# Pre norms of a chain of fp32 layers: products of x times the norm's gain, a token's factor applied out of PSUM, squares from PSUM, and one program without barriers

## The chip, the core and the metric

The kernel runs on one core of a Trainium2 chip. The metric is the device time of one execution in microseconds (us); lower is better. Its engines are TensorE (PE) with its weight loads (PEld), VectorE (DVE), ScalarE (ACT), GpSimd (POOL) and SyncE (SP), which issues the transfers. They run their own programs and meet at semaphores.

## The reference

x is 512 tokens by 1024 columns in float32. Two `hybrid_layer`s run over it and then one `hybrid_layer_2`, each between norms:

```python
def rms_norm(x, g):
    y = xf * lax.rsqrt(jnp.mean(xf * xf, axis=-1, keepdims=True) + EPS)
    return (y * g.astype(jnp.float32)).astype(x.dtype)

def hybrid_layer(x, ...):
    h = rms_norm(x, g_mix_pre)
    u = h @ w_in
    ...                         # attention, convolution and retention of slices of u
    mix = jnp.concatenate([y_att, y_conv, y_ret], axis=-1) @ w_out
    x = x + rms_norm(mix, g_mix_post)
    h = rms_norm(x, g_mlp_pre)
    f = jnp.square(jax.nn.relu(h @ w_up)) @ w_down
    return x + rms_norm(f, g_mlp_post)

def hybrid_layer_2(x, mem, ...):
    x = x + 0.5 * swiglu_ffn(rmsnorm(x, ffn1_norm), ffn1_w_in, ffn1_w_down)
    u = rmsnorm(x, mix_norm)
    proj = u @ w_in
    ...                         # a state space scan, dilated attention, attention over mem, gates
    x = x + merged @ w_out
    x = x + 0.5 * swiglu_ffn(rmsnorm(x, ffn2_norm), ffn2_w_in, ffn2_w_down)
    return x

def swiglu_ffn(x, w_in, w_down):
    a, b = jnp.split(x @ w_in, 2, axis=-1)
    return (jax.nn.silu(a) * b) @ w_down
```

The result is `rmsnorm` of it with `final_norm`. A *pre norm* stands ahead of a projection (`g_mix_pre`, `g_mlp_pre`, `ffn1_norm`, `ffn2_norm`), a *post norm* behind one. The factor `rsqrt(mean)` of a norm is one number per token, so it can be applied to the rows of `h @ w` as well as to h.

## The kernel before

**Layout.** Everything is feature-major: x is `x_sb`, 8 tiles k of 128 features by 512 tokens. A projection takes a tile's features from the weights and leaves 128 outputs by 512 tokens in one PSUM bank; there are four (`gemm0` to `gemm3`), taken in turns by twos.

**Products.** An fp32 product is three matmuls of rounded parts: high by high, high by low, low by high. The weights come in *pieces* of 256 columns and 8 tiles of rows, 1 MB each. A piece is loaded by SP into `w_raw` (two buffers, `load_block` L325), rounded by ACT to `w_hi` (`round_block`, L344), and DVE makes `w_lo` (`rest_block`, L353). A piece has two output tiles m; `product` (L356, its matmuls at L384) runs m outside and k inside: 48 matmuls. It waits for `w_lo` once (semaphore `w_rest`) and, in a stage's first piece, for each tile of h (`h_ready`). Two pieces are in work at a time: a buffer is loaded again when both parts of the piece in it are made, and rounded again when the products of the piece before are done (`units`). `g_free` counts the banks read out.

**A norm** is a chain across the engines: squares on ACT (`norm_squares`, L456); their sum over features on PE by products with a matrix of ones into PSUM (`norm_add`, L461, and L482), 8 of them, or 3 where POOL has added the first six squares (`squares_added`, L471); ACT's root of one row (`norm_rooted`, L510); PE turns the row into columns (`norm_turn`, L498); DVE's reciprocal (L515); PE spreads it over all partitions (`norm_spread`, L504). Then, for a post norm, DVE scales each tile of `out_sb` by gain and factor (L520) and adds it to x (L549). For a pre norm DVE scales each tile of x by gain and factor into `out_sb` (L520), ACT rounds it to `h_hi` (L527), DVE subtracts to `h_lo` (L538), and the product of that tile may start.

**Stages of a layer.** 14 pieces of w_in with attention, convolution and retention woven in, 4 pieces of w_out, and twice 8 pieces of up and 8 of down. Up is relu by ACT out of PSUM (L1005), square on DVE (L1216), rounding. The second down half's tiles are copied from PSUM by ACT to `part` (L1017) and added by DVE (L1239). In the third part each FFN is 11 pairs of pieces (a silu on the first, a copy of the second, their product on DVE), then down with `part` and an add (L2043).

**Order around the norms.** All queues are written by hand. At w_out's and down's end PE does `norm_of_added` for the post norm and then `norm_total` for the pre norm, which both run before any product of the next stage. The two layers are one loop (`nc.Fori(0, DEPTH)`) with a block in it; at its end, and behind the start block, `clear_counts` puts all semaphores to zero between barriers, and the weight buffers' first two pieces, loaded and rounded ahead, are told to the next block by `head_start`. The third part is a block of its own. The start block loads constants and x, then weights; it does the first pre norm's root and both roundings.

## Time and profile before

| | us |
|---|---|
| three runs, median (lowest, highest) | 2854.04 (2852.43, 2858.58) |
| the profiled execution | 2853.72 |
| its span, first to last instruction | 2851.9 |
| PE busy in the span | 2710.3 (95%) |
| DVE, ACT, POOL busy | 1291.4 (45%), 1015.0 (36%), 287.8 (10%) |

The mean granted clock of PE is 0.972 of full speed. The boundaries between stages, where a pre norm stands, with PE's busy time in each (a stretch from about the last tile of the old stage to the second piece of the new one):

| stretch, us | boundary | length | PE busy |
|---|---|---|---|
| 0 to 57 | start | 57 | 36.0 |
| 324 to 375 | w_out to up, layer 0 | 51 | 41.9 |
| 701 to 762 | layer 0 to layer 1 | 61 | 42.1 |
| 1029 to 1082 | w_out to up, layer 1 | 53 | 44.5 |
| 1408 to 1466 | layer 1 to third part | 58 | 43.3 |
| 2458 to 2500 | w_out2 to ffn2 | 42 | 32.8 |

How to read the rows below: a row of the page's first part is an engine's busy time with its share of the span. A busy PE isn't PE at its peak: matmuls are pipelined, each is shown with 0.39 us at the full clock, and they start 0.2265 us apart. A granted clock of 0.50 is the lower of its two levels, 1.2 of 2.4 GHz.

### The profile page before, as it was taken

How to read it: one execution, taken by the hardware profiler on the slowest of the kernel's cores; microseconds unless marked ns; L12 is line 12 of the kernel's file. 1: busy time of each engine (PE TensorE's matmuls, PEld its weight loads, DVE VectorE, ACT ScalarE, POOL GpSimd, SP SyncE). 2: the span in 40 equal slices, each digit the busy share in tenths (PEclk: the TensorE clock that was granted, in tenths of full speed). 3: DMA queues.
4: the chain of work that ended last, by engine and by line, in shares of the span. 5: the costliest groups of instructions: out<-in, count | busy, mean ns of one | idle time of the engine just before them, and what ended most of it. 6: DMA issues, size and time to landing. Idle time of an engine off the chain costs nothing. (4 is left out here: it accounts for less than half of the span.)

```text
span 2851.9 us, 31899 instructions
## 1 busy us (share of the span) xinstructions
PE 2710.3 (95%) x12330; PEld 2122.2 (74%) x12330; DVE 1291.4 (45%) x1666; ACT 1015.0 (36%) x1433; POOL 287.8 (10%) x276
## 2 busy tenths in 40 slices
PE   7999899999799989999989999999999998899998
PEld 5875688887587568888768888777777666688886
DVE  4754442342574444233343333478773446333322
ACT  3333332232333333233333333433235453334322
POOL 0000000001000000000100000067540230000000
PEclk9999999999899989999999999999999999999999
DMA  3310122322231012322122322412131024122222
GB/s 123 126 53 30 59 82 95 104 88 74 72 122 45 30 59 88 103 89 103 59 82 96 103 92 91 168 60 74 53 132 52 30 75 162 61 101 90 94 91 80
DMA packets 41443, 241.88 MB, mean 85 GB/s; under 512 B 5232, under 2 KB 5744, under 8 KB 18416
## 3 DMA queue, kind: packets, MB, share of 16 engines
q1 hardware_dynamic: 41056, 239.25, 24.4%
q8 instruction: 77, 1.26, 0.2%
q0 software_dynamic: 272, 1.05, 0.1%
q14 instruction: 38, 0.31, 0.0%
HBM read 231.90 MB, written 8.39 MB: 84 GB/s over the span
## 5 line engine op out<-in xcount | busy, mean ns | idle before, releaser
L353 DVE TENSOR_TENSOR w_lo<-w_raw,w_hi 128x2048 fp32r<-128x2048 f32 (+3 forms) x219 | 464.2, 2120 | 850.4 <-ACT w_hi L344 850.2
L384 PE MATMUL gemm<-h_hi,w_hi 128*128 128x512 f32 x1936 | 777.7, 402 | 47.9 <-DVE h_lo L538 44.0
L384 PE MATMUL gemm<-h_hi,w_lo 128*128 128x512 f32 x1936 | 760.5, 393 | 0.0
L384 PE MATMUL gemm<-h_lo,w_hi 128*128 128x512 f32 x1936 | 760.5, 393 | 0.0
L344 ACT ACTIVATE w_hi<-w_raw 128x2048 fp32r<-128x2048 f32 (+3 forms) x219 | 383.5, 1751 | 257.5 <-PE gemm L384 254.3
L384 PEld LDWEIGHTS gemm<-h_hi,w_hi 128*128 128x128 f32 x1936 | 367.0, 190 | 139.0 <-issue 46.1
L384 PEld LDWEIGHTS gemm<-h_hi,w_lo 128*128 128x128 f32 x1936 | 367.2, 190 | 78.2
L384 PEld LDWEIGHTS gemm<-h_lo,w_hi 128*128 128x128 f32 x1936 | 368.1, 190 | 71.8 <-issue 1.7
L384 PE MATMUL gemm<-f_hi,w_hi 128*128 128x512 f32 x512 | 199.4, 389 | 0.0
L384 PE MATMUL gemm<-f_hi,w_lo 128*128 128x512 f32 x512 | 199.4, 389 | 0.0
L384 PE MATMUL gemm<-f_lo,w_hi 128*128 128x512 f32 x512 | 199.4, 389 | 0.0
L1770 ACT ACTIVATE swi<-gemm 128x512 f32<-128x512 f32 x88 | 52.7, 598 | 285.3 <-PE gemm L384 285.3
L384 PE MATMUL gemm<-g_hi,w_hi 128*128 128x512 f32 x352 | 137.5, 390 | 0.0
L384 PE MATMUL gemm<-g_lo,w_hi 128*128 128x512 f32 x352 | 137.1, 389 | 0.0
L384 PE MATMUL gemm<-g_hi,w_lo 128*128 128x512 f32 x352 | 137.1, 389 | 0.0
L1216 DVE TENSOR_TENSOR tt<-tt 128x512 f32<-128x512 f32 x64 | 44.1, 689 | 156.3 <-ACT tt L1005 156.3
L1005 ACT ACTIVATE tt<-gemm 128x512 f32<-128x512 f32 x64 | 38.3, 599 | 207.7 <-PE gemm L384 207.7
L384 PEld LDWEIGHTS gemm<-f_hi,w_lo 128*128 128x128 f32 x512 | 96.1, 188 | 19.9
L384 PEld LDWEIGHTS gemm<-f_hi,w_hi 128*128 128x128 f32 x512 | 96.1, 188 | 19.9
L384 PEld LDWEIGHTS gemm<-f_lo,w_hi 128*128 128x128 f32 x512 | 96.1, 188 | 19.9
L471 POOL TENSOR_TENSOR sq_f<-sq_f 128x512 f32<-128x512 f32 x20 | 31.1, 1557 | 778.0 <-ACT sq_f L456 776.8
L384 PE MATMUL gemm<-w_hi,h_hi 128*128 128x256 f32 (+1 forms) x352 | 107.3, 305 | 0.0
(370 smaller groups left out, 3614.4 us busy)
## 6 DMA issues: line engine op xcount, KB each, us to landing
w_raw<-in_w SPq DMA_DIRECT2D x171, 1024.0 KB, 4.8
w_raw<-in_w SPq DMA_DIRECT2D x16, 768.0 KB, 4.2
w_raw<-in_w SPq DMA_DIRECT2D x16, 640.0 KB, 3.8
w_raw<-in_w SPq DMA_DIRECT2D x18, 512.0 KB, 3.7
bias_t<-in_att_bias SPq DMA_DIRECT2D x2, 1536.0 KB, 9.2
decay_t<-in_c_decay SPq DMA_DIRECT2D x2, 1536.0 KB, 8.2
x_sb<-in_x SPq DMA_DIRECT2D x4, 512.0 KB, 5.4
x_kept<-x_sb SPq DMA_DIRECT2D x1, 2048.0 KB, 11.0
```

Of the source, the lines that this page charges most:

```text
L344: act.activation(w_hi[:, b.slot, 0:size], w_raw[:, b.slot, 0:size], ACT.Copy).then_inc(S["w_rounded"], 1)
L353: dve.tensor_tensor(w_lo[:, b.slot, 0:size], w_raw[:, b.slot, 0:size], w_hi[:, b.slot, 0:size].bitcast(F32), ALU.subtract).then_inc(S["w_r ...
L384: mm = pe.matmul(dst, lhs, rhs, start=b.first and k == 0 and j == 0, stop=b.last and k == b.kt - 1 and j == 2)
L471: pool.tensor_tensor(sq[:, 0, :], sq[:, 0, :], sq[:, k, :], ALU.add).then_inc(S["sq_added"], 1)
L1005: act.activation(tt[:, 2 * j + m, :], tile_of(b, m), ACT.Relu).then_inc(S["g_free"], 1)
L1216: dve.tensor_tensor(tt[:, 2 * j + m, :], tt[:, 2 * j + m, :], tt[:, 2 * j + m, :], ALU.mult).then_inc(S["f_sq"], 1)
L1770: act.activation(swi[:, 2 * j + m, :], tile_of(b, m), (ACT.Silu, ACT.Copy)[j]).then_inc(S["g_free"], 1)
```

## The change

Four things change, in one edit of the whole program.

1. *Pre norms at the head of a stage* (mix_pre, mlp_pre, ffn1, ffn2). ACT makes `h_hi` from x times gain (`raw_hi`), DVE `h_lo` (`raw_rest`), as soon as a tile of x is there, with no token factor. `opening` puts the products of the stage's first two pieces one tile k at a time, alternating between the pieces, and the norm's sum, turn and spread among the last of them. ACT copies the spread factor into `rs` (`open_act`). POOL adds six of the squares in all of these norms. The pre norms of the mix in the third part and of mem stay as they were.
2. *The factor* is applied to the results. In the layers' w_in, DVE multiplies the first two pieces out of PSUM, POOL the q, k, rq, rk and rg tiles in SBUF (`by_root`), and the token-major pieces get it as ACT's scale. In up, DVE takes relu and factor out of PSUM in one instruction and ACT squares. In the third part's FFNs DVE multiplies the first piece by the factor out of PSUM, ACT takes the silu, POOL multiplies by the factor again, and DVE multiplies with the second piece out of PSUM.
3. *PSUM is read directly* for the squares of w_out and for the adds of the last down tiles (`part` goes), which DVE now does before the next `rest_block`.
4. *One program.* The layers are written out twice in one block, each with offsets for its semaphore counts (`counts`), the pieces of all parts have one numbering, the layers' parameters have two buffers, and `clear_counts`, `head_start` and the barriers go. At the start SP issues the parameters and the first piece before x.

The new functions, and the places that use them (indentation and counts that only follow are left out):

```diff
+        def raw_hi(act, k, gain):
+            act.activation(h_hi[:, k, :], x_sb[:, k, :], ACT.Copy, scale=gain[:, k:k + 1]).then_inc(S["norm_hi"], 1)
+        def raw_rest(dve, j, k, gain):
+            dve.wait_ge(S["norm_hi"], KD * j + k + 1)
+            dve.scalar_tensor_tensor(out=h_lo[:, k, :], in0=x_sb[:, k, :], scalar=gain[:, k:k + 1],
+                                     in1=h_hi[:, k, :].bitcast(F32), op0=ALU.mult,
+                                     op1=ALU.subtract).then_inc(S["h_ready"], 1)
+        def post_norm_dve(dve, i, gain, normed, j, next_gain):
             norm_inverse(dve, i)
-            for k in range(KD + 1):
-                if k < KD:
+            for k in range(KD):
                     norm_scale(dve, i, k, out_sb, out_sb, gain)
                 if k:
-                    dve.wait_ge(S["normed"], KD * i + k)
-                    dve.tensor_tensor(x_sb[:, k - 1, :], x_sb[:, k - 1, :], out_sb[:, k - 1, :],
-                                      ALU.add).then_inc(S["x_done"], 1)
-        gains = {n: par[:, 8 * i:8 * i + 8] for i, n in enumerate(("mix_pre", "mix_post", "mlp_pre", "mlp_post"))}
-        conv_w = par[:, 32:94].rearrange("p (j t) -> p j t", j=2)
-        conv_b, ln_g, ln_b = par[:, 94:96], par[:, 96:98], par[:, 98:100]
+                    raw_rest(dve, j, k - 1, next_gain)
+                dve.wait_ge(S["normed"], normed + k + 1)
+                dve.tensor_tensor(x_sb[:, k, :], x_sb[:, k, :], out_sb[:, k, :], ALU.add).then_inc(S["x_done"], 1)
+            raw_rest(dve, j, KD - 1, next_gain)
+        def split_x(act, i, sq, gain, wait, tiles=range(KD)):
+            for k in tiles:
+                act.wait_ge(wait[0], wait[1] + k + 1)
+                raw_hi(act, k, gain)
+                act.activation(sq[:, k, :], x_sb[:, k, :], ACT.Square).then_inc(S["squares"], 1)
+        OPENING = [(q, k) for k in range(5) for q in range(2)] + [
+            (0, 5), (0, 6), (0, 7), "sum", (1, 5), "turn", (1, 6), "spread", (1, 7)]
+        FIRST_OPENING = [(0, k) for k in range(6)] + [
+            (1, 0), (1, 1), (0, 6), (0, 7), "sum", (1, 2), (1, 3), (1, 4), "turn", (1, 5), (1, 6), "spread", (1, 7)]
+        def opening(pe, pair, i, sq, ready, order=OPENING):
+            waited = 0
+            for at in order:
+                if at == "sum":
+                    added_total(pe, i, sq)
+                elif at == "turn":
+                    norm_turn(pe, i)
+                elif at == "spread":
+                    norm_spread(pe, i)
+                else:
+                    b, k = pair[at[0]], at[1]
+                    if k == 0:
+                        pe.wait_ge(S["w_rest"], b.n + 1)
+                    if k >= waited:
+                        pe.wait_ge(S["h_ready"], ready + k + 1)
+                        waited = k + 1
+                    wh, wl = view(w_hi, b), view(w_lo, b)
+                    for m in range(b.tiles):
+                        if k == 0 and b.need[m]:
+                            pe.wait_ge(S["g_free"], b.need[m])
+                        c = slice(m * P, (m + 1) * P)
+                        dst = bank[b.bank + m][:]
+                        pe.matmul(dst, wh[:, k, c], h_hi[:, k, :], start=k == 0, stop=False)
+                        pe.matmul(dst, wh[:, k, c], h_lo[:, k, :], start=False, stop=False)
+                        mm = pe.matmul(dst, wl[:, k, c], h_hi[:, k, :], start=False, stop=k == KD - 1)
+                        if k == KD - 1:
+                            mm.then_inc(S["units"], 1)
+        def open_act(act, i, b):
+            round_block(act, b.n + 2)
+            norm_rooted(act, i)
+            act.wait_ge(S["norm_spread"], i)
+            act.activation(rs[:], t_ps[:], ACT.Copy).then_inc(S["rs_ready"], 1)
+        def open_dve(dve, i, b):
+            norm_inverse(dve, i)
+            rest_block(dve, b.n + 2)
...
+        def begin_sync(sp):
+            sp.dma_start(pars[0][:, 0:100], A["par1"][0]).then_inc(first_par_in, 16)
+            load_block(sp, plan[0])
+            load_x(0)
             sp.dma_start(ones[:], A["c_ones"]).then_inc(consts_in, 16)
             sp.dma_start(ident[:], A["c_ident"]).then_inc(consts_in, 16)
+            load_x(2)
+            load_x(4)
+            load_block(sp, plan[1])
+            load_x(6)
...
-                    norm_of_added(pe, 1, 0, sq_f)
-                    norm_total(pe, 2, out_sb)
+            norm_of_added(pe, N0 + 1, sq_f)
...
+                    opening(pe, plan1[first.i:first.i + 2], N0 + 2, out_sb, cnt("h_ready", 2 * KD))
...
-                    norm_of_added(pe, 3, KD - 3, sq_f)
-                    norm_total(pe, 4, sq_f)
+            norm_of_added(pe, N0 + 3, sq_f)
...
+            def by_root(b, tiles):
+                for m in range(b.tiles):
+                    pool.wait_ge(S["g_free"], b.t0 + m + 1)
+                    pool.tensor_tensor(tiles[m], tiles[m], rs[:], ALU.mult).then_inc(S["pool_r"], 1)
...
-                    squares_added(pool, 1, 0, sq_f)
-                    squares_added(pool, 3, KD - 3, sq_f)
+            squares_added(pool, N0 + 1, sq_f)
+            squares_added(pool, N0 + 2, out_sb)
+            squares_added(pool, N0 + 3, sq_f)
+            squares_added(pool, N0 + 4, sq_f)
...
-                    norm_squares(act, 3, out_sb, sq_f, wait=(S["part_done"], 0), tiles=(KD - 2, KD - 1))
-                    norm_rooted(act, 3)
-
-                    round_next(act, 0, plan1)
-                    norm_squares(act, 4, x_sb, sq_f, wait=(S["x_done"], KD))
-                    norm_rooted(act, 4)
-                    round_next(act, 1, plan1)
+            for b in plan1[DOWN[1]:DOWN[1] + 8]:
+                round_block(act, b.n + 2)
+                k = (b.i - DOWN[1]) // 2 * 2 - 2
+                if not b.last and k >= 0:
+                    norm_squares(act, N0 + 3, out_sb, sq_f, wait=(S["g_free"], last_down), tiles=(k, k + 1))
+            norm_squares(act, N0 + 3, out_sb, sq_f, wait=(S["g_free"], last_down), tiles=(KD - 2, KD - 1))
+            norm_rooted(act, N0 + 3)
+            split_x(act, N0 + 4, sq_f, next_gain, (S["x_done"], cnt("x_done", KD)))
...
+                for m in range(2):
+                    dve.wait_ge(S["units"], t.u(b.u0 + m + 1))
+                    dve.scalar_tensor_tensor(out=tt[:, 2 * j + m, :], in0=tile_of(b, m), scalar=0.0, in1=rs[:],
+                                             op0=ALU.max, op1=ALU.mult).then_inc(S["g_free"], 1)
...
+                        dve.tensor_tensor(out_sb[:, k, :], out_sb[:, k, :], tile_of(b, m),
+                                          ALU.add).then_inc(S["g_free"], 1)
+                rest_block(dve, b.n + 2)
...
-            clear_counts()
...
+            def silu_by_root(base):
+                with pool.Fori(0, 11) as i:
+                    for m in range(2):
+                        pool.wait_ge(S["silu"], base + i * 2 + (m + 1))
+                        pool.tensor_tensor(swi[:, m, :], swi[:, m, :], rs[:], ALU.mult).then_inc(S["silu_r"], 1)
```

How the order of the instructions changes on two engines. First DVE between w_out and up of a layer (L353 and after it L357 are the weights' low parts, L520 and then L494 the scale, L549 and then L534 the add to x, L538 and then L522 the low part of h). Before, the post norm's rows and the beginning of the pre norm's:

```order
L353 TENSOR_TENSOR w_lo<-w_raw,w_hi 128x2048 x4
L515 RECIPROCAL tiny<-mixed 128x4
L520 SCALAR_TENSOR_TENSOR out_sb<-out_sb,par_sb,turned 128x512 x2
L549 TENSOR_TENSOR x_sb<-x_sb,out_sb 128x512
L520 SCALAR_TENSOR_TENSOR out_sb<-out_sb,par_sb,turned 128x512
...
L549 TENSOR_TENSOR x_sb<-x_sb,out_sb 128x512 x2
L515 RECIPROCAL tiny<-mixed 128x4
L520 SCALAR_TENSOR_TENSOR out_sb<-x_sb,par_sb,turned 128x512 x2
L538 TENSOR_TENSOR h_lo<-out_sb,h_hi 128x512
```

And after the change:

```order
L357 TENSOR_TENSOR w_lo<-w_raw,w_hi 128x2048 x4
L489 RECIPROCAL tiny<-mixed 128x4
L494 SCALAR_TENSOR_TENSOR out_sb<-out_sb,par_sb,turned 128x512
L534 TENSOR_TENSOR x_sb<-x_sb,out_sb 128x512
L494 SCALAR_TENSOR_TENSOR out_sb<-out_sb,par_sb,turned 128x512
L522 SCALAR_TENSOR_TENSOR h_lo<-x_sb,par_sb,h_hi 128x512
L534 TENSOR_TENSOR x_sb<-x_sb,out_sb 128x512
...
L534 TENSOR_TENSOR x_sb<-x_sb,out_sb 128x512
L522 SCALAR_TENSOR_TENSOR h_lo<-x_sb,par_sb,h_hi 128x512
L489 RECIPROCAL tiny<-mixed 128x4
```

The low part of h has moved from behind the second reciprocal to one row behind each add of the post norm.

The same place on PE, the sums and the first products, before:

```order
L482 MATMUL mixed<-sq_f_86,ones_sb_57 128x512
L461 MATMUL mixed<-sq_f_86,ones_sb_57 128x512 x2
L498 MATMUL mixed<-ones_sb_57,rs_60 128x1 x4
L504 MATMUL turned<-ident_sb_56,tiny_62 128x128 x4
L461 MATMUL mixed<-out_sb_55,ones_sb_57 128x512 x8
L498 MATMUL mixed<-ones_sb_57,rs_60 128x1 x4
L504 MATMUL turned<-ident_sb_56,tiny_62 128x128 x4
L384 MATMUL gemm0<-h_hi_53,w_hi_50 128x512
```

After, first where the opening begins and then its last part:

```order
L472 MATMUL mixed<-ones_sb_57,rs_60 128x1 x4
L478 MATMUL turned<-ident_sb_56,tiny_63 128x128 x4
L572 MATMUL gemm0<-h_hi_53,w_hi_50 128x512
L573 MATMUL gemm0<-h_lo_54,w_hi_50 128x512
L574 MATMUL gemm0<-h_hi_53,w_lo_51 128x512
L572 MATMUL gemm1<-h_hi_53,w_hi_50 128x512
...
L465 MATMUL mixed<-out_sb_55,ones_sb_57 128x512
L437 MATMUL mixed<-out_sb_55,ones_sb_57 128x512 x2
L572 MATMUL gemm2<-h_hi_53,w_hi_50 128x512
...
L472 MATMUL mixed<-ones_sb_57,rs_60 128x1 x4
...
L478 MATMUL turned<-ident_sb_56,tiny_63 128x128 x4
```

The eight ones-products of the pre norm have become three (L465, L437), and they stand 78 rows of products behind the start of the stage, before the second piece's last three tiles.

The third place is DVE from the last piece of w_out2 into ffn2 (L2043 and then L2456 are the adds to x). Before:

```order
L353 TENSOR_TENSOR w_lo<-w_raw,w_hi 128x2048
L2043 TENSOR_TENSOR x_sb<-x_sb,part 128x512 x2
L515 RECIPROCAL tiny<-mixed 128x4
L520 SCALAR_TENSOR_TENSOR out_sb<-x_sb,par_sb,turned 128x512 x2
L538 TENSOR_TENSOR h_lo<-out_sb,h_hi 128x512
```

And after:

```order
L357 TENSOR_TENSOR w_lo<-w_raw,w_hi 128x2048
L2456 TENSOR_TENSOR x_sb<-x_sb,gemm 128x512 x2
L522 SCALAR_TENSOR_TENSOR h_lo<-x_sb,par_sb,h_hi 128x512 x2
L489 RECIPROCAL tiny<-mixed 128x4
L357 TENSOR_TENSOR w_lo<-w_raw,w_hi 128x2048
L2131 TENSOR_TENSOR swi<-gemm,rs 128x512 x2
L2138 TENSOR_TENSOR swi<-gemm,swi 128x512 x2
```

The adds now read the banks themselves, so a bank is free behind the weights' low part and the add; each pair of adds is followed by two low parts of h.

## Rows read from the trace of the kernel before

**Rows 1.** The page's head line and the busy share of PE, first part.

```profile
span 2851.9 us, 31899 instructions
...
PE 2710.3 (95%) x12330; PEld 2122.2 (74%) x12330; DVE 1291.4 (45%) x1666; ACT 1015.0 (36%) x1433; POOL 287.8 (10%) x276
```

**Rows 2.** Waits of PE by releaser: us in total, times, longest.

```profile
PE gemm L384 <- DVE h_lo L538: 44.0, 20, 12.9
```

**Rows 3.** Stretches: length; PE, PEld, DVE, ACT, POOL busy (count); clock; DMA; GB/s.

```profile
375.00:700.00 325.00, 325.00 (x1435) 269.23 (x1434) 109.74 (x95) 99.89 (x109) 9.11 (x5) 1.00 0.27 94
701.00:762.00 61.00, 42.08 (x152) 27.69 (x151) 28.36 (x38) 21.65 (x29) 0.00 (x0) 0.80 0.16 54
```

**Rows 4.** Timeline (start, us, engine, line), layer 0, w_out to up; idle before in brackets.

```profile
324.27 0.60 ACT L886 ACTIVATE out_sb<-gemm 128x512 f32<-128x512 f32 x1 [4.84 <-PE gemm L384]
325.44 1.98 PE L461 MATMUL mixed<-sq_f,ones_sb 128*128 128x512 f32 x4 [0.34 <-ACT sq_f L456]
...
327.60 0.66 ACT L510 ACTIVATE rs<-mixed,eps_c 1x512 f32<-1x512 f32 x1
...
330.17 1.16 PE L504 MATMUL turned<-ident_sb,tiny 128*128 128x128 f32 x8 [0.81 <-DVE tiny L515]
331.37 1.41 DVE L520 SCALAR_TENSOR_TENSOR out_sb<-out_sb,par_sb,turned 128x512 f32<-128x512 f32 x2 [1.25 <-PE turned L504]
332.69 0.68 DVE L549 TENSOR_TENSOR x_sb<-x_sb,out_sb 128x512 f32<-128x512 f32 x1
...
349.20 0.77 PE L384 MATMUL gemm<-h_hi,w_hi 128*128 128x512 f32 x1 [2.32 <-DVE h_lo L538]
...
374.78 0.60 ACT L1005 ACTIVATE tt<-gemm 128x512 f32<-128x512 f32 x1 [4.84 <-PE gemm L384]
```

**Rows 5.** Timeline, layer 0 to layer 1.

```profile
708.03 1.41 DVE L520 SCALAR_TENSOR_TENSOR out_sb<-out_sb,par_sb,turned 128x512 f32<-128x512 f32 x2 [1.65 <-PE turned L504]
...
736.40 0.76 PE L384 MATMUL gemm<-h_hi,w_hi 128*128 128x512 f32 x1 [12.85 <-DVE h_lo L538]
...
761.99 0.60 ACT L886 ACTIVATE cg<-gemm 128x512 f32<-128x512 f32 x1 [4.84 <-PE gemm L384]
```

**Rows 6.** Stretches of PE alone: length, busy (matmuls), clock, DMA, GB/s.

```profile
736.40:739.40 3.00, 3.00 (x7) 0.50 0.92 358
739.40:742.40 3.00, 2.90 (x9) 0.71 0.67 276
```

**Rows 7.** Timeline, the other boundaries: start's end; layer 1; third part.

```profile
57.16 0.60 ACT L886 ACTIVATE cg<-gemm 128x512 f32<-128x512 f32 x1 [4.84 <-PE gemm L384]
...
1037.46 0.75 DVE L520 SCALAR_TENSOR_TENSOR out_sb<-out_sb,par_sb,turned 128x512 f32<-128x512 f32 x1 [2.17 <-PE turned L504]
...
1081.82 0.60 ACT L1005 ACTIVATE tt<-gemm 128x512 f32<-128x512 f32 x1 [4.84 <-PE gemm L384]
...
1415.52 0.75 DVE L520 SCALAR_TENSOR_TENSOR out_sb<-out_sb,par_sb,turned 128x512 f32<-128x512 f32 x1 [2.10 <-PE turned L504]
...
1466.22 0.60 ACT L1770 ACTIVATE swi<-gemm 128x512 f32<-128x512 f32 x1 [4.84 <-PE gemm L384]
```

**Rows 8.** Transfers, 0 to 20 us: GB/s in 40 slices of 0.5 us.

```profile
GB/s 0 0 0 77 109 106 205 291 360 418 360 365 324 385 381 373 328 323 257 428 442 360 492 442 360 475 410 407 287 139 19 0 0 0 0 0 0 0 0 0
```

**Rows 9.** Timeline, w_out2 to ffn2.

```profile
2458.68 0.60 ACT L1756 ACTIVATE part<-gemm 128x512 f32<-128x512 f32 x1 [3.80 <-PE gemm L384]
2459.17 1.90 ACT L344 ACTIVATE w_hi<-w_raw 128x2048 fp32r<-128x2048 f32 x1
2461.11 2.29 DVE L353 TENSOR_TENSOR w_lo<-w_raw,w_hi 128x2048 fp32r<-128x2048 f32 x1 [7.38 <-ACT w_hi L344]
...
2499.55 0.60 ACT L1770 ACTIVATE swi<-gemm 128x512 f32<-128x512 f32 x1 [4.84 <-PE gemm L384]
```

**Rows 10.** Timeline, POOL and DVE side by side in layer 0's w_out.

```profile
314.59 2.73 POOL L471 TENSOR_TENSOR sq_f<-sq_f 128x512 f32<-128x512 f32 x2 [8.86 <-ACT sq_f L456]
...
316.87 2.60 DVE L353 TENSOR_TENSOR w_lo<-w_raw,w_hi 128x2048 fp32r<-128x2048 f32 x1 [8.99 <-ACT w_hi L344]
```

More of the change, by code:

```diff
@@ L75, in __init__, with number @@
         self.group, self.narrow = group, narrow
-def number(pieces, tok_tiles=None):
+def number(*parts):
+    pieces = []
+    for part in parts:
+        for i, b in enumerate(part):
+            b.i = i
+            pieces.append(b)
     units = 0
@@ L214, in third_pieces @@
     ffn("ffn2")
[L215 to L216 removed]
+    return out, start
 def build(nc, ins, outs):
     A = ins
[L221 to L222 removed]
+    third_part, AT2 = third_pieces()
+    plan = number(*(layer_pieces() for _ in range(DEPTH)), third_part)
+    n1 = (len(plan) - len(third_part)) // DEPTH
+    plan2 = plan[DEPTH * n1:]
     with ExitStack() as ctx:
```

3018 lines of the change are left out of this document (1527 added, 1491 removed).

## The prediction

> **What bounds the kernel now.** I read the head line and the busy shares first [rows 1]: TensorE (PE) works through 95% of a span of 2851.9 us and no other engine through half of it, so only time in which PE waits, or works on something that goes away, can be won. Then the waits by releaser: PE's largest is that of the products at line 384 for the low part of h at line 538, 44.0 us in 20 waits [rows 2]. Then two stretches [rows 3]: from 375 to 700 us (up and down of a layer) PE is busy throughout at a full clock; from 701 to 762 (a layer's end and the next one's first two pieces) for 42.1 of 61 us, at a mean clock of 0.80. The time lies at the boundaries, so I read those row by row.
>
> At each boundary I use anchors that stay in the changed kernel: T0, where ScalarE (ACT) takes the last-but-one tile of the old stage out of PSUM; t0, the first scale of the post norm on VectorE (DVE); and the end, the take-out of the last-but-one tile of the new stage's second piece. From w_out to up in layer 0 [rows 4] T0 is 324.27, then come three ones-products (0.99 each: 1.98 for two), the root at 327.60, the spread at 330.17, t0 at 331.37. Eight times scale and add follow, in which PE only sums the pre norm's squares; then root, turn and spread again; the first product starts at 349.20, the end is 374.78. Of these 50.5 us the two pieces need 21.7: 96 matmuls at 325.00/1435 = 0.2265 us each [rows 3].
>
> **The change, part by part.**
>
> *An opening.* Products take x times gain, which is there as soon as x is, and the pre norm's sum, turn and spread stand among the products of the second piece. On PE, from its first product to the end: 96 x 0.2265 = 21.7; three ones-products, 3.0 (eight become three, GpSimd (POOL) adds the first six squares); the spread 1.16 [rows 4] and the turn, eight small loads too, as much: 27.0. After a long wait PE's clock is at its lower level (1.2 of 2.4 GHz): at 736.40, 16 products take 6.00 us at granted clocks of 0.50 and 0.71 where 3.6 would do [rows 6], 2.4 lost. The new idle time ahead is shorter, so I take 1.7: **28.7** an opening. Bounds: 27.0 (no slow clock, and nothing below it, since the same products remain) and 31 (slow for twice as long).
>
> *Its start.* Per tile DVE makes a scale, a low part (new, two SBUF operands, bounded by the 0.68 of the add) and the add: 0.70 + 0.68 + 0.68, about 2.05 us; ACT makes the high part (0.60 as a copy) and the square beside it. The first low part stands behind scale, add, high part and the next scale: t0 + 2.9. PE eats 2.72 us of products a tile (12 of them), so DVE keeps ahead; tiles 5 to 7 are taken at 1.36 each, where its lead is 2 us at a full clock, 4 at a slow start.
>
> *B0, w_out to up, layer 0.* Squares now come from PSUM ahead of the copy: 0.55 sooner. Start 331.37 - 0.55 + 2.9 = 333.7, end 362.4 for 374.78: **12.3**. *B1, the same in layer 1* [rows 7]: 1037.46 - 0.55 + 2.9 + 28.7 = 1068.5 for 1081.82: **13.3**.
>
> *C0, layer 0 to layer 1.* t0 708.03, first product 736.40, end 761.99 [rows 5]; the barrier, the clearing of the counts and the branch lie in the 12.85 us that PE waits there, and go too. ACT now rounds a piece (1.90) ahead of the last squares, 0.75 on the root. 708.03 + 0.75 + 2.9 + 28.7 = 740.4: **21.6**. *C1, layer 1 to the third part* [rows 7]: 1415.52 + 32.35 = 1447.9 for 1466.22: **18.3**.
>
> *A, the start.* Before, all squares, a root and two roundings stand ahead of the products, end 57.16 [rows 7]. After, gains and first piece are asked for first. Summing the half-microsecond slices [rows 8], some 1.3 MB are in by 6.6 us, and piece 0 (1.05 MB, asked for first) with them; then ACT's rounding 1.90, DVE's low part 2.29 [rows 9], and x's low part 0.7: start 11.6, end 40.3: **16.9**, give or take 2 for what the queue does with another order.
>
> *E, w_out2 to ffn2.* T0 2458.68, end 2499.55 [rows 9]. h's tiles are made while w_out2 still runs, and PE goes on with tile 0 of piece 0 at once. Then it waits for piece 1's low part (rounding from T0 on, 1.90, then 2.29 on DVE, so T0 + 4.3) and for banks that the last adds free behind it on DVE (T0 + 5.6). That leaves some 3.8 idle: T0 + 3.8 + 27.0 + 0.4 = 2489.9: **9.7**.
>
> *F, the final norm.* Its adds read PSUM and save one copy, 0.60: **0.5**.
>
> *The factor elsewhere.* POOL multiplies q, k, rq, rk and rg by it (15 tiles a layer), DVE the first two pieces and up (relu and factor in one instruction). In the third part's FFNs a pair's first piece goes DVE product 0.7, ACT silu 0.6, POOL product 1.4 twice: done 4.8 us after that piece, where the second piece ends after 10.9 (48 x 0.2265). From there DVE's two products, ACT's rounding, two low parts and the next weights' low part are about 5.8 of the next 10.9. DVE and ACT are busy for a third of the long stretch (109.74 and 99.89 of 325 us [rows 3]). So **0**, hidden behind PE's products; if the cover were gone it is rival 3. The unrolled layers, the offsets of the counts and the one numbered plan add nothing on an engine in use: **0**.
>
> Sum: 12.3 + 13.3 + 21.6 + 18.3 + 16.9 + 9.7 + 0.5 = 92.6. From the profiled execution's 2853.7 (1.8 over its span, 0.3 below the runs' median) that is **2761 us**.
>
> **A rule against this change.** Two POOL adds of squares, 1.37 us each, end at 317.32; a weights' low part that DVE starts at 316.87 takes 2.60 us, the like one at 2461.11 with POOL idle 2.29 [rows 9, 10]: 0.31 lost on 0.45 of overlap. The changed kernel puts five such adds beside each opening's DVE chain. The Trainium skill, "SBUF — State Buffer", section "Who interferes with whom", says that a DVE instruction with two SBUF inputs and a GpSimd instruction that reads SBUF shut each other out, the one issued second waiting in full. By that rule the five adds would stop the chain for as long as they last; the row agrees in sign and roughly in size. What that gives is rival 1.
>
> **The rivals.**
>
> (1) *Openings starved or cold.* If the five adds (6.8 us) stop DVE for their whole length, its chain loses 6.8 against a lead of 4: up to 2.8 in each of B0, B1, C0, C1, +11, so 2772. If only the clash of the two SBUF kinds counts (two thirds of DVE's time), 4.5 against 4: +2. And if the clock stays low for 8 us, six openings lose some 1.7 more: +10, 2771. Both in part: 2767 to 2780. For it: rows 10, and the mean clock of 0.80 [rows 3]; against: in half of its time POOL waits for the next square. Chance 0.28.
>
> (2) *More is won.* PE's wait ahead of the products shrinks from 12.85 us [rows 5] to about 2.5; if the clock is then up, 5 x 1.7 = 8.5 less, and the start may be 2 sooner: 2749 to 2755. Against it: after 2.32 us of wait the product at 349.20 still takes 0.77 and not 0.39. Chance 0.17.
>
> (3) *POOL becomes the third part's bound: slower.* There are 22 FFN pairs, and each now goes through POOL. A pair loses time from the point at which its POOL products end 10.9 + (10.9 - 5.8) = 16 us after its first piece, where they end at 4.8 now. To eat 92.6 us it takes 4.2 a pair more, 20.2 us: a POOL product of 9 us each and not 1.37 [rows 10]. Past that, it is slower than before, over 2860. Chance 0.02; as much again, 0.02, that such a product takes 8 to 9 us and the gain is just eaten.
>
> (4) *The products do not open.* Piece 1's low part, or the four banks that two interleaved pieces hold at once, could be late until every tile is there anyhow. Then PE starts at t0 + 17.3 (8 x 2.05 + 0.9) and ends 27.0 later: B0 nothing, B1 0.7, C0 761.99 - 753.1 = 8.9, C1 5.6, start 11, E 9.7, together 36: 2818. Against it: the post norm waits for the sum of squares anyhow, and into the 7.1 us from T0 to t0 a rounding and a low part (1.90 + 2.29) fit. Chance 0.01.
>
> **How the numbers follow.** The forecast, 2755 to 2767, gets 0.50 and is the likeliest: 2761. To hold 8 in 10 the range goes to 2749 (rival 2, the clock up in all openings and an early start) and to 2780 (rival 1; openings at their bound of 31 are +14). What it leaves out are rivals 3 and 4 and the far ends of 1 and 2. A measurement of this kernel can tell about 0.2%, 6 us, from no change: faster by more than that 0.50 + 0.28 + 0.17 + 0.01 = 0.96, within it 0.02, slower 0.02.
>
> **What would show it.** After: the first product of up some 9.5 us behind T0, and products from there without a gap of over 0.5 us; the three ones-products within the second piece; from t0 to the end 31.6 us in B and C where C0 had 54.0; no barrier at layer ends; the start's end near 40; PE busy throughout between boundaries. Wrong: PE waiting for h's low part at tiles 5 to 7 beside POOL adds (rival 1), a clock of 0.50 for over 4 us (rival 1) or never (rival 2), PE waits inside the third part's FFN pairs (rival 3), a first product 17 us behind t0 (rival 4). The forecast fails as a whole if ends move less than starts.

## The result, and the profile after

The changed kernel takes 2774.35 us (median of 4 runs, 2773.67 to 2774.83) for 2853.89 us: a ratio of 0.9718, 95% interval 0.9703 to 0.9734. That is 79.5 us less, where 92.6 were forecast, and it lies in the range of 2749 to 2780: not in the forecast's own stretch of 2755 to 2767, but in the one of 2767 to 2780 that the first rival had. The profiled execution took 2773.67 us, its span:

```profile
span 2771.8 us, 31517 instructions
...
PE 2669.7 (96%) x12280; PEld 2109.0 (76%) x12280; DVE 1342.1 (48%) x1670; ACT 944.5 (34%) x1331; POOL 428.3 (15%) x375
```

PE is busy 40.6 us less than in [rows 1] and idle for about as much less; POOL has half as much again to do. The waits of PE by releaser (total, times, longest):

```profile
PE gemm L572 <- DVE h_lo L522: 17.6, 9, 12.5
PE gemm L572 <- issue: 12.6, 4, 3.2
```

The 44.0 us of [rows 2] are 17.6, of which 12.5 are the start. The 12.6 us put down to "issue" are four waits of 3.15 between a post norm's spread and the first product.

One correction to the prediction's words before the numbers: it calls its anchors T0 and end the take-out of the *last-but-one* tile. The rows show the *last* tile (all 96 products of the two pieces lie ahead of 374.78, and the ones-products begin at 324.07). The arithmetic used them so, and nothing in the sum changes. Below, T0 is the start of the first ones-product of the post norm, and the end is the first product of the stage's third piece; both are 0.2 us ahead of those of the rows. A's T0 is the start of the span. E has no post norm; its T0 is where w_out2's last product gives way, 2458.5 before and 2386.7 after.

| boundary | T0 to end, before | after | won | forecast |
|---|---|---|---|---|
| A, start | 57.0 | 41.8 | 15.2 | 16.9 |
| B0, w_out to up, layer 0 | 50.5 | 41.7 | 8.8 | 12.3 |
| C0, layer 0 to 1 | 60.8 | 42.2 | 18.6 | 21.6 |
| B1, w_out to up, layer 1 | 52.4 | 41.7 | 10.7 | 13.3 |
| C1, layer 1 to third part | 58.0 | 42.0 | 16.0 | 18.3 |
| E, w_out2 to ffn2 | 40.9 | 32.5 | 8.4 | 9.7 |
| all | | | 77.7 | 92.1 |

Between the boundaries another 2.4 us went, most of them in layer 1's w_in (1.7) and the third part (1.2); no wait of PE there changed by as much, and what they are stays open. They may be chance: in pe_sum below, whose edit doesn't touch it, the third part between its two openings is 5.0 us longer than here. So the order of the terms came out as forecast, and every one was taken too large. The boundary w_out to up of layer 0 shows why. Its timeline, first up to the first product (start, duration, engine, line; idle time before in brackets):

```profile
309.12 1.02 PE L465 MATMUL mixed<-sq_f,ones_sb 128*128 128x512 f32 x2
...
312.08 0.66 ACT L484 ACTIVATE rs<-mixed,eps_c 1x512 f32<-1x512 f32 x1
...
314.66 2.07 PE L478 MATMUL turned<-ident_sb,tiny 128*128 128x128 f32 x8 [0.82 <-DVE tiny L489]
...
316.78 0.75 DVE L494 SCALAR_TENSOR_TENSOR out_sb<-out_sb,par_sb,turned 128x512 f32<-128x512 f32 x1 [2.17 <-PE turned L478]
...
319.04 0.75 DVE L522 SCALAR_TENSOR_TENSOR h_lo<-x_sb,par_sb,h_hi 128x512 fp32r<-128x512 f32 x1
...
319.89 0.77 PE L572 MATMUL gemm<-h_hi,w_hi 128*128 128x512 f32 x1 [3.15 <-issue]
```

The spread takes 2.07 us for 1.16 in [rows 4]: PE's clock has already fallen there (the granted clock is 0.50 from 314.6). It is at its lower level for the first products as well (stretches: length; PE, PEld, DVE, ACT, POOL busy; clock):

```profile
319.89:322.89 3.00, 3.00 (x7) 2.42 (x8) 2.87 (x4) 1.24 (x2) 1.15 (x1) 0.50 0.00 0
322.89:325.89 3.00, 3.00 (x10) 2.33 (x10) 2.87 (x4) 1.24 (x2) 1.10 (x2) 0.68 0.00 0
```

And this is DVE's chain beside POOL's adds, and what PE sees of it later:

```profile
319.70 0.69 DVE L534 TENSOR_TENSOR x_sb<-x_sb,out_sb 128x512 f32<-128x512 f32 x1
...
321.74 1.32 POOL L454 TENSOR_TENSOR out_sb<-out_sb 128x512 f32<-128x512 f32 x1 [21.34 <-ACT out_sb L542]
321.85 1.77 DVE L534 TENSOR_TENSOR x_sb<-x_sb,out_sb 128x512 f32<-128x512 f32 x1
323.54 0.73 DVE L494 SCALAR_TENSOR_TENSOR out_sb<-out_sb,par_sb,turned 128x512 f32<-128x512 f32 x1
...
338.19 0.50 PE L572 MATMUL gemm<-h_hi,w_hi 128*128 128x512 f32 x1 [0.74 <-DVE h_lo L522]
...
340.33 0.50 PE L572 MATMUL gemm<-h_hi,w_hi 128*128 128x512 f32 x1 [0.48 <-DVE h_lo L522]
```

The add to x at 319.70 takes 0.69 us; the one at 321.85, issued 0.11 behind POOL's, takes 1.77: it stands until POOL is done at 323.06 and then runs. This isn't chance. POOL's add waits for ACT's square, which ends just as DVE comes to the add of x, so it falls on that add in five tiles of each opening. PE waits for tiles 6 and 7: 0.74 and 0.48 us idle in these rows, and 1.5 to 1.7 us an opening in all four by the starts of its products.

At the start ACT's table load has moved behind the first wait (before, it ran at 0.73 us, under the transfers). Of A's missing 1.7 us it is 1.0, as the run `ends` shows below; the rest lies in the opening, 29.3 us for 28.7:

```profile
6.12 1.28 ACT L348 ACT_TABLE_LOAD   x1 [6.12 <-DMA w_raw<-in_w]
7.41 1.91 ACT L348 ACTIVATE w_hi<-w_raw 128x2048 fp32r<-128x2048 f32 x1
```

### The profile page after: what moved, and what is told of

Read it like the earlier page. It is cut to its first block, busy times and chain, and to the rows that moved or that the text cites. A ratio compares the mean times of both kernels' runs of the same rounds, so it can differ in the third digit from the quotient of the medians.

```text
span 2771.8 us, 31517 instructions
## 1 busy us (share of the span) xinstructions
PE 2669.7 (96%) x12280; PEld 2109.0 (76%) x12280; DVE 1342.1 (48%) x1670; ACT 944.5 (34%) x1331; POOL 428.3 (15%) x375
## 4 chain that ended last, share of the span: by engine, by line
PE 87%; DVE 7%; ACT 4%; issue 2%; DMA 0%; ACTq 0%; DVEq 0%; SPq 0%
PE gemm L388 71%; ACT w_hi L348 2%; DVE x_sb L534 2%; PE score L742 1%; PE mixed L763 1%; DVE w_lo L357 1%; PE gemm L572 1%; DVE h_lo L522 1%; PE mixed L1601 1%; ACT h_hi L517 1%; PE gemm L574 1%; PE score L1590 1%; PE gemm L573 1%; PE turned L753 1%; PE mixed L437 1%
## 5 line engine op out<-in xcount | busy, mean ns | idle before, releaser
L357 DVE TENSOR_TENSOR w_lo<-w_raw,w_hi 128x2048 fp32r<-128x2048 f32 (+3 forms) x225 | 473.2, 2103 | 651.0 <-ACT w_hi L348 650.7
L388 PE MATMUL gemm<-h_hi,w_lo 128*128 128x512 f32 x1744 | 679.9, 390 | 0.0
L388 PE MATMUL gemm<-h_lo,w_hi 128*128 128x512 f32 x1744 | 679.1, 389 | 0.0
L348 ACT ACTIVATE w_hi<-w_raw 128x2048 fp32r<-128x2048 f32 (+3 forms) x225 | 393.4, 1749 | 438.9 <-PE gemm L388 401.0
L388 PEld LDWEIGHTS gemm<-h_hi,w_hi 128*128 128x128 f32 x1744 | 327.6, 188 | 75.8 <-issue 6.1
L388 PEld LDWEIGHTS gemm<-h_hi,w_lo 128*128 128x128 f32 x1744 | 327.3, 188 | 69.2
L388 PEld LDWEIGHTS gemm<-h_lo,w_hi 128*128 128x128 f32 x1744 | 327.8, 188 | 66.1 <-issue 1.7
L454 POOL TENSOR_TENSOR sq_f<-sq_f 128x512 f32<-128x512 f32 x30 | 47.7, 1590 | 750.6 <-ACT sq_f L432 653.1
L1749 POOL TENSOR_TENSOR swi<-swi,rs 128x512 f32<-128x512 f32 x44 | 56.9, 1295 | 411.3 <-ACT swi L1857 411.3
L572 PE MATMUL gemm<-h_hi,w_hi 128*128 128x512 f32 x192 | 85.7, 446 | 33.9 <-DVE h_lo L522 17.6
L388 PE MATMUL gemm<-w_lo,h_hi 128*128 128x256 f32 (+1 forms) x352 | 106.0, 301 | 0.0
## 6 DMA issues: line engine op xcount, KB each, us to landing
x_kept<-x_sb SPq DMA_DIRECT2D x1, 2048.0 KB, 10.9
```

Source lines behind the costliest of these rows:

```text
L348: act.activation(w_hi[:, b.slot, 0:size], w_raw[:, b.slot, 0:size], ACT.Copy).then_inc(S["w_rounded"], 1)
L357: dve.tensor_tensor(w_lo[:, b.slot, 0:size], w_raw[:, b.slot, 0:size], w_hi[:, b.slot, 0:size].bitcast(F32), ALU.subtract).then_inc(S["w_r ...
L388: mm = pe.matmul(dst, lhs, rhs, start=b.first and k == 0 and j == 0, stop=b.last and k == b.kt - 1 and j == 2)
L454: pool.tensor_tensor(sq[:, 0, :], sq[:, 0, :], sq[:, k, :], ALU.add).then_inc(S["sq_added"], 1)
L572: pe.matmul(dst, wh[:, k, c], h_hi[:, k, :], start=k == 0, stop=False)
L1749: pool.tensor_tensor(swi[:, m, :], swi[:, m, :], rs[:], ALU.mult).then_inc(S["silu_r"], 1)
```

## The experiments

Eleven kernels ran, each timed against the kernel before in turns on one chip. Times are medians in us; the ratio is to the kernel before. The changed kernel itself has 0.9718. The kernels ran on three chips, on which the kernel before took 2852.7 us (pe_sum, sq_r, warm, best0), 2854.0 (warm_sq, ends, serial, blocks) and 2849.7 (pool3, pool6, best1), and 2853.9 beside the changed kernel; so across these groups the ratios compare, and times only to some us. Where times are close I go by the places in the profile. Two causes were in question for what was missing, and they can hide each other: POOL's adds hold DVE up (lockout), and PE's clock falls because PE stands idle ahead of an opening (idle clock). The plain rival to both is that the chain from ACT to DVE is just slower than I took it.

### pe_sum: POOL's adds out of the openings

```diff
                 if at == "sum":
-                    added_total(pe, i, sq)
+                    for k in range(KD):
+                        norm_add(pe, i, sq, k)
...
-            squares_added(pool, N0 + 2, out_sb)
...
-            squares_added(pool, N0 + 4, sq_f)
```

> The changed kernel, but in the four openings behind a post norm PE sums all eight squares itself and GpSimd adds none. Theory (GpSimd's add shuts DVE out for its whole length): the add to x goes back from 1.78 to 0.69 us in all tiles, the tile period of DVE's chain from 3.24 to about 2.1 us, and PE no longer waits for h's low part at tiles 6 and 7 (1.6 us an opening now). PE pays five more ones-products of 0.72 us: 3.6 - 1.6 = 2.0 more in each of four, so about 2782 us. Rival (the chain is slow of itself, by its own waits from ACT to DVE and back): the waits stay and the time is 4 x 3.6 up, 2789 us.

Measured: 2786.07 us, ratio 0.9762 (0.9746 to 0.9779). By time alone this lies between the theory's 2782 and the rival's 2789. The waits decide: those for h's low part in the four openings are gone, all of them, and only the start's is left (total, times, longest):

```profile
PE gemm L577 <- DVE h_lo L524: 12.6, 1, 12.6
```

The group of the adds to x (line, count, busy, mean ns), first of the changed kernel and then of this one:

```profile
L534 DVE TENSOR_TENSOR x_sb<-x_sb,out_sb 128x512 f32<-128x512 f32 x32 | 43.8, 1368 | 0.1
```

```profile
L536 DVE TENSOR_TENSOR x_sb<-x_sb,out_sb 128x512 f32<-128x512 f32 x32 | 21.9, 685 | 0.1
```

21.9 us of DVE's time were lockout: 20 adds by 1.09 us. DVE lost nothing else. The time went up by more than the 8 us expected, since five further ones-products cost 4.3 us in an opening (0.86 each) and not 3.6. Less the 1.6 of the waits that is 2.7; the four openings are 2.1 to 2.8 us longer, 9.8 together, and a spread at the lower clock at layer 0's end adds 0.9.

### sq_r: the squares rounded, all eight summed by PE

```diff
-                act.activation(sq[:, k, :], x_sb[:, k, :], ACT.Square).then_inc(S["squares"], 1)
+                act.activation(as_r(sq, k), x_sb[:, k, :], ACT.Square).then_inc(S["squares"], 1)
...
+                        mm = pe.matmul(o_ps[0:32, :], ones_r[:], as_r(sq, k), start=k == 0, stop=k == KD - 1)
```

(`as_r` is the same place as fp32r, `ones_r` a rounded matrix of ones; again no POOL adds there.)

> As the one before, but ACT writes these squares rounded (fp32r) and PE sums all eight at 0.23 us each, 1.8 us for the three fp32 ones-products' 2.2. Theory of the lockout: no wait for h's low part, 1.6 + 0.4 less in each of four openings, 2766 us. Rival (chain slow of itself): only 0.4 less in each, 2773 us.

Measured: 2766.14 us, ratio 0.9693 (0.9677 to 0.9709). The first product to the end of an opening is 28.0 to 28.4 us for 30.9. That is 2.5 to 3.1 less and not 2.0: a part of the slow products goes too, since PE no longer stops at tiles 6 and 7 and starts again. The one wait left for h's low part is again the start's:

```profile
PE gemm L587 <- DVE h_lo L532: 12.6, 1, 12.6
```

The rival (chain slow of itself) falls with these two runs: its times were 2789 and 2773, and no opening waits.

### warm: work for PE in its waits

```diff
             added_total(pe, i, sq)
+            busy(pe, 6)
             norm_turn(pe, i)
+            busy(pe, 2)
             norm_spread(pe, i)
+            busy(pe, 12)
+
+        def busy(pe, n):
+            for _ in range(n):
+                pe.matmul(s_ps[0][:, 0:P], ones[:], ident[:], start=True, stop=True)
```

> The changed kernel, with small ones-products of 128 columns that nobody reads put on PE in its waits around the post norm: 6 ahead of the turn, 2 ahead of the spread, 12 behind it. Theory (the clock falls because PE has nothing to do there): the spread takes 1.2 instead of 2.1 us, t0 comes 0.9 us sooner in four places, and the opening's first products follow at 0.23 instead of 0.43 us. But the DVE chain with GpSimd's adds still gives tile 7 when it does, so what PE wins ahead it waits at tiles 5 to 7: about 2770 us, with PE's waits for h's low part up from 1.6 to about 4 us an opening. Rival (the clock falls for another reason): nothing moves, 2774 us, or some us more if the extra products delay the turn.

Measured: 2774.32 us, ratio 0.9725 (0.9709 to 0.9741): the same as without them, and the rival's number, not the 2770 of the theory. But the clock did what the theory said. The same three microseconds from the first product of layer 0's up, for 7 products at 0.50 above (PE alone: length, busy, clock):

```profile
319.60:322.60 3.00, 3.00 (x13) 1.00 0.00 0
```

And the waits of PE for h's low part over the whole run:

```profile
PE gemm L580 <- DVE h_lo L530: 23.2, 18, 13.1
```

17.6 in 9 waits have become 23.2 in 18: 2.8 to 3.2 us an opening by the starts of the products, for 1.5 to 1.7. Layer 0's opening of up takes 30.92 us in both. A PE at full speed only comes sooner to a DVE that POOL holds up: DVE, not PE, sets the end of these openings. The 0.9 us of t0 was won at w_out to up (6.75 from T0 to t0 for 7.66) and lost at the layer ends (8.61 for 8.01), where the small products stood in the way of the turn.

### warm_sq: both

> Rounded squares on PE and the small products in PE's waits, without the three small edits. The squares alone gave 8.2 us, the small products alone nothing. If the two causes hide each other (a PE at full speed only waits for a DVE that GpSimd holds up), together they give more than their sum: four openings at about 26.1 us for 28.1 with the squares alone, and 0.9 at two of the spreads, 2756 us. Rival (the small products never gain anything, and the rest of the best kernel's gain is from its three edits): 2766 us.

Measured: 2755.91 us, ratio 0.9656 (0.964 to 0.9672). An opening is 26.1 us, and T0 to end at w_out to up 35.9 for 41.7. The squares alone won 8.2 us, the small products alone 0, both 18.4 (by the ratios 7.1, -2.0 and 17.7). So the squares count alone, and the small products only behind them: lockout and idle clock are shown to be the two causes of the four long openings. The clock there (PE alone):

```profile
317.54:320.54 3.00, 3.00 (x13) 1.00 0.00 0
```

### ends: three small edits

```diff
-                opening(pe, plan2[up:up + 2], i0, sq, ready)
+                opening(pe, plan2[up:up + 2], i0, sq, ready, OPENING if name == "ffn1" else FIRST_OPENING)
...
             act.wait_ge(eps_made, 2)
+            act.activation(tiny[:, 40:41], quarter[:], ACT.Copy)
             round_block(act, 0)
...
-                round_block(act, b.n + 2)
+                if b.i < DOWN[1] + 7:
+                    round_block(act, b.n + 2)
...
             norm_squares(act, N0 + 3, out_sb, sq_f, wait=(S["g_free"], last_down), tiles=(KD - 2, KD - 1))
+            round_block(act, plan1[DOWN[1] + 7].n + 2)
             norm_rooted(act, N0 + 3)
```

> The changed kernel with the three small edits alone. ffn2's opening takes piece 0 ahead, so the 3.9 us wait for the last add of w_out2 goes, and with it the slow clock behind it (some 1.6): 5.5 us. The table load ahead of the first wait: 1.2 us. The last squares ahead of ACT's rounding at the two layer ends: PE's 1.7 us wait for them goes, but the openings there are then as starved as before: 1.7 each. Together 10 us, 2764 us. If one of them only moves a wait, it shows at its place: the start's end (41.80 now), T0 to end of the two layer ends (42.2 and 42.0 now), ffn2's opening (32.45 now).

Measured: 2765.07 us, ratio 0.9687 (0.9671 to 0.9703), span 2764.5 for 2771.8. By place: the start's end comes 1.0 us sooner. ffn2's opening takes 26.7 us for 32.5: this wait of the changed kernel is gone, and the slow products behind it.

```profile
2391.97 0.47 PE L572 MATMUL gemm<-h_hi,w_hi 128*128 128x512 f32 x1 [3.72 <-DVE x_sb L2456]
```

At the layer ends only 0.1 and 0.0 of the hoped 1.7 each. So the places give 7.0 us of the 7.3 by which the span is shorter; that the time comes near the 2764 expected, for which 10 us were worked out, is in part luck. The timeline of layer 0's end in this kernel:

```profile
679.61 0.66 ACT L484 ACTIVATE rs<-mixed,eps_c 1x512 f32<-1x512 f32 x1
679.73 2.29 DVE L357 TENSOR_TENSOR w_lo<-w_raw,w_hi 128x2048 fp32r<-128x2048 f32 x1 [2.50 <-ACT w_hi L348]
...
681.94 0.17 DVE L489 RECIPROCAL tiny<-mixed 128x4 f32<-128x4 f32 x1
...
682.17 2.06 PE L478 MATMUL turned<-ident_sb,tiny 128*128 128x128 f32 x8 [0.80 <-DVE tiny L489]
```

The root comes 1.5 us sooner after T0 (3.3 for 4.8). But DVE has the weights' low part in front of the reciprocal, from 679.73 for 2.29 us, and that now sets the turn; and PE, idle for longer, does the spread at the lower clock (2.06; in the changed kernel 1.16 at this place). One wait taken away, and the weights' low part and the slow spread in its place.

### serial: the pieces of an opening one after the other

```diff
-        OPENING = [(q, k) for k in range(5) for q in range(2)] + [
-            (0, 5), (0, 6), (0, 7), "sum", (1, 5), "turn", (1, 6), "spread", (1, 7)]
+        OPENING = [(0, k) for k in range(KD)] + [(1, k) for k in range(5)] + [
+            "sum", (1, 5), "turn", (1, 6), "spread", (1, 7)]
```

> The changed kernel with the two pieces of an opening one after the other (all tiles of piece 0, then piece 1), in the openings behind the start's. PE then needs a tile every 1.36 us and gets one every 3.24 (with GpSimd's adds), so it waits for h's low part in piece 0: tile 7 is ready 20.4 us after the first product, and 1.36 + 10.9 + 4.7 follow: 37.4 us for 30.9 now, in four openings, and 4 us less in ffn2's, whose wait for the bank falls away: about 2796 us. Rival (interleaving by tile is worth nothing, since PE makes up for it in piece 1): 2774 less 4, 2770 us.

Measured: 2795.64 us, ratio 0.9792 (0.9775 to 0.9808). Layer 0's opening of up takes 37.7 us, with PE idle for 1.6 us at each of tiles 3 to 6. So interleaving by tile is worth 6.8 us an opening here; ffn2's opening gets 5.8 back, as in ends.

```profile
PE gemm L572 <- DVE h_lo L522: 40.3, 24, 12.5
```

### blocks: the program cut into three again

```diff
-        with nc.Block() as block:
...
+        for stage in range(DEPTH + 1):
+            in_block(stage)     # a block each: start and layer 0, layer 1, third part
```

(SP loads the next stage's first two pieces at the end of each block, as the others ask for them there.)

> The changed kernel cut into three blocks (start and layer 0, layer 1, third part) with the barrier between them that ends a block, counts and everything else as they are. The barrier holds PE until DVE's and ACT's post norm chain has ended, so the two openings behind it start 20 us later but find all tiles ready (no starving, 1.6 less), and the barrier itself costs 1 or 2: 20 us for each of the two layer ends, 2814 us. So most of the difference between the layer ends and the w_out boundaries would be what the barrier keeps from overlapping, not the barrier. Rival (one program is worth its barriers alone): 2778 us.

Measured: 2815.08 us, ratio 0.9862 (0.9845 to 0.9878). Both boundaries show PE waiting at the block's end, and at layer 0's end the post norm's last low part of h stands just ahead of PE's first product:

```profile
PE gemm L572 <- PEq L2480: 47.7, 2, 23.9
```

```profile
708.09 0.75 DVE L522 SCALAR_TENSOR_TENSOR h_lo<-x_sb,par_b,h_hi 128x512 fp32r<-128x512 f32 x1 [0.79 <-ACT h_hi L517]
...
709.34 0.77 PE L572 MATMUL gemm<-h_hi,w_hi 128*128 128x512 f32 x1 [23.88 <-PEq L2480]
```

From t0 to the first product it is 23.8 us (685.50 to 709.34) and not 3.1, and only 0.5 of them come behind DVE's last row (708.84). So of all the 79.5 us some 41 hang on there being no barrier at the two layer ends, and nearly all of that is overlap and not the barrier's own time.

### pool3 and pool6: does POOL bound the third part?

```diff
                         pool.wait_ge(S["silu"], base + i * 2 + (m + 1))
+                        for q in range(1):      # pool6: range(2)
+                            pool.wait_ge(S["spare_s"], 1 * (base + i * 2 + m) + q + 1)
+                            pool.tensor_tensor(swi[:, 4:7, :], rs_3, rs_3, ALU.mult).then_inc(S["spare_s"], 1)
```

(`rs_3` stands for `rs` read three times; in pool6 the count is 2 times the bracket.)

> The changed kernel with one more GpSimd product ahead of each of its 44 products in the third part's FFNs: three tiles at once into a spare place that nobody reads, some 3.9 us. This is for the rival that GpSimd bounds the third part. By the prediction's arithmetic GpSimd's two products then end 4.8 + 2 x 3.9 = 12.6 us behind the pair's first piece, against a limit of 16: nothing is lost, 2774 us. If GpSimd's lockout of DVE counts as well (its last product beside the weights' low part and DVE's low parts), the limit is lower by up to 3.9 and a part of 22 x 0.5 us shows: up to 2785.

> Two such extra products ahead of each: 4.8 + 4 x 3.9 = 20.4 us against the limit of 16, 4.4 us in each of 22 pairs, some 97 us: 2871 us, slower than the kernel before. That is the price at which the rival of the bound on GpSimd was put (a product of 9 us). If it comes out under 2830, DVE or ACT make up for it in a way that the arithmetic leaves out; over 2900, the lockout of DVE adds to it.

Measured: pool3 2785.9 us, ratio 0.9776 (0.9759 to 0.9792); pool6 2819.81 us, ratio 0.9895 (0.9878 to 0.9911). Both forecasts missed: pool3 is over its 2774 and just over the 2785 that it had for a lockout in every pair, and pool6 is 51 us under its 2871. Against the changed kernel they lose 11.6 and 45.5 us by time, 16.6 and 50.5 by the ratios. The groups of POOL in pool6:

```profile
L1753 POOL TENSOR_TENSOR swi<-rs 128x1536 f32<-128x1536 f32 x88 | 276.4, 3141 | 196.0 <-ACT swi L1864 192.5
L1756 POOL TENSOR_TENSOR swi<-swi,rs 128x512 f32<-128x512 f32 x44 | 60.7, 1379 | 0.0
```

An extra product took 3.1 us and not 3.9, so pool6 ends its products 4.8 + 4 x 3.14 = 17.4 us behind the first piece, 1.4 over the limit of 16. In the pairs in the middle of both FFNs PE then waits 0.5 us (0.7 with the slower restart), and 3.2 at the first piece of down. The limit was about right, if 0.7 us too low. What the arithmetic left out is the pair *behind an opening*: there both pieces end at once, and POOL's products don't have the second piece's 10.9 us to hide in. In pool3 and pool6 it waits 3.7 and 9.4 us, with a slow clock behind it:

```profile
PE gemm L388 <- DVE w_lo L357: 37.3, 22, 9.4
```

(The row is of pool6 and counts both FFNs, with 4.0 us that the changed kernel has too.) So two places, not 22, decide first. In pool3 these two waits, 3.7 each with 1.9 of slow products, are 11.3 of the 12.5 us by which its span is longer, so the lockout in every pair isn't what it shows. For the rival itself: even a POOL product of 7.7 us leaves the kernel 1% faster than before; the rival was priced near enough and did not come.

### best0 and best1: the fastest version

best0 is sq_r, warm and ends together; best1 has `busy(pe, 5)` at the start too, behind the wait for the constants.

> Rounded squares summed by PE, the small products in PE's waits, and three small edits: ffn2 opens in the order of the first opening (piece 0 ahead, for the 3.9 us wait for the bank there), ACT's table is loaded at the start before its first wait (1.3 us), at layer ends the last squares come ahead of the rounding (0.7 us in each of two). If lockout and idle clock are both right, they add up here and more: 8 us from the squares, 4 x 3.5 from the clock, since now DVE keeps ahead of PE at full speed, 3.7 + 1.3 + 1.5 from the three: about 2746 us. If only the lockout is right: 2760. If neither: 2768.

> The best kernel (2746.2 us) with five small products on PE at the start as well, between the arrival of the constants (about 8.1 us) and the first product at 11.3. The first opening has 3.9 us of slow products there. If five small products of 0.6 us at the slow clock are enough, up to 2.5 of them go: 2744 us. Rival (the clock needs longer than there is time ahead of the first product): the slow products stay or shrink by under 1 us, 2746 us.

Measured: best0 2746.18 us (2745.14 to 2746.95), ratio 0.9622 (0.9606 to 0.9638), 28.2 us faster than the changed kernel. best1 2748.14 us, ratio 0.9644 (0.9628 to 0.966), 0.0022 above best0's: nothing was won, and its rival was right. PE of best1 at the start:

```profile
8.34 2.50 PE L478 MATMUL score<-ident_sb,ones_sb 128*128 128x128 f32 x10 [8.34 <-DMA ident_sb<-in_c_ident]
...
11.66 0.77 PE L595 MATMUL gemm<-h_hi,w_hi 128*128 128x512 f32 x1 [0.82 <-DVE h_lo L540]
```

The lower pace ends at 17.4 us in both. In best0 no opening behind the start's waits for h, and the layer ends' edit now pays: T0 to t0 is 7.0 us for 8.6 in warm_sq, where ends alone had 7.9, with its spread at the lower clock.

## Why the prediction was right, and where it was too large

- *The number*: 2761 was forecast and 2774 came. The range held because rival 1 was in it. The sum itself is 13 us too large, and without the 2.4 us between the boundaries, which no term had, it would be 15.
- *The bound, and where the time would go*: right. PE's work between boundaries kept its length, the gains lie at the six boundaries in the forecast order, and the factor elsewhere cost nothing that shows. In the third part's pairs DVE's product that reads PSUM runs beside POOL's without a loss:

```profile
1396.74 2.55 POOL L1749 TENSOR_TENSOR swi<-swi,rs 128x512 f32<-128x512 f32 x2 [16.00 <-ACT swi L1857]
1398.14 0.69 DVE L2138 TENSOR_TENSOR swi<-gemm,swi 128x512 f32<-128x512 f32 x1 [2.10 <-POOL swi L1749]
```

- *The opening at 28.7 us*: 30.9 to 31.1 in B and C. Three parts of that term: the sum, turn and spread cost 4.7 and not 5.3; slow products cost 2.8 to 3.1 and not 1.7 (some 2.4 for 12 products at 0.43 us, the rest behind each stop); tiles 6 and 7 wait 1.5 to 1.7, where I took nothing.
- *The failing step* is the one "so DVE keeps ahead": its period was priced at 2.05 us from rows of DVE alone, and beside POOL it is 3.24. The prediction had the row for it [rows 10] and rival 1 had the mechanism and nearly its price ("the five adds (6.8 us) stop DVE for their whole length", up to 2.8 an opening; measured 5.4 on the chain, 1.6 at PE). What I had wrong is the argument against it, "in half of its time POOL waits for the next square": that wait is what sets the clash, since a wait chain that meets at the same point in each tile overlaps every time. The Trainium skill, "SBUF — State Buffer", section "Who interferes with whom", says of a DVE instruction with two SBUF inputs and a GpSimd instruction that reads SBUF that they contend for one read interface, under an exclusive lock. The rows agree as far as they go: 1.77 for 0.69 behind a POOL add that was issued first, and no loss for the instruction with a PSUM operand.
- *t0*: forecast 0.55 us sooner after T0 at w_out to up. In layer 1 it came so, 7.66 for 8.21; in layer 0 it is 7.66 for 7.30, 0.36 later. The root did come sooner there (2.96 for 3.53 behind T0), and the reciprocal, which stands behind the weights' low part on DVE in both kernels, with it (5.32 for 5.87), but the spread lost 0.9 to the clock, which it had kept before in layer 0 and not in layer 1 [rows 4, 7]. At the layer ends 0.75 later was forecast for the rounding, and 0.96 and 0.51 came.
- *A*: 15.2 for 16.9, 1.0 of it the table load. *E*: 8.4 for 9.7: the wait is 3.9 where 3.8 was worked out, but it also brings slow products (some 2 us in this opening), which the term took at 0.4. *F*: nothing for 0.5; the spread there was slow as well, 1.75 us for 1.17 before.
- *Rival 2* (the clock stays up): wrong for this kernel; warm shows that work on PE keeps it up, and that this is worth nothing here as long as POOL holds DVE up.
- *Rivals 3 and 4* did not come. pool3 and pool6 put a price on rival 3. serial and blocks show what rival 4 would have cost in parts: with either the tiles or the boundary held back, the kernel is 21 and 41 us slower and still faster than before.

## What to carry to other kernels

A token's factor can be taken out of a projection, and what that wins is not the scale but the order: products may start with the first tile of x, and the norm's chain runs under them, as long as no barrier stands between. When such a chain feeds PE tile by tile, price each step beside what runs on the other engines at that moment; a helper on GpSimd that waits for the same tiles met VectorE at the same instruction here in every opening, five times each. And if two causes hold the end, taking one of them away may show nothing in the time: look at whether the waits have moved, then take both.
